# Dividing the attended rows instead of the probabilities, and copying the second tile's turned rows on VectorE

## The reference, cut to what matters

```python
m = jnp.max(s, -1, keepdims=True)
p = jnp.exp(s - m)
den = jnp.sum(p, -1, keepdims=True)
o = jnp.einsum('bdhnqk,bdhnkc->bdhnqc', (p / den).astype(v.dtype), vw)
```

## Time and profile before

| | us |
|---|---|
| median of 3 runs | 2731.94 |
| the three runs | 2727.18, 2731.94, 2734.06 |
| the profiled execution | 2726.64 |
| its span, first to last instruction | 2724.8 |

### The profile page before, as it was taken

How to read it: one execution, slowest core, us unless ns; L and a number is a source line. 1 busy time by engine, 2 the same in 40 slices (tenths; PEclk the granted TensorE clock), 3 DMA queues, 4 the chain that set the end, 5 groups by cost and what they waited for, 6 DMA issues and landing times.

```text
span 2724.8 us, 49556 instructions
## 1 busy us (share of the span) xinstructions
PE 2635.3 (97%) x20658; PEld 2060.4 (76%) x20658; DVE 1841.1 (68%) x2227; ACT 1556.5 (57%) x1989; POOL 228.5 (8%) x217
## 2 busy tenths in 40 slices
PE   8999999996799999999999999999999999999997
PEld 8898777774677777777777777777777777777765
DVE  4331388757777677767766776777677667767788
ACT  3102488621566666666666666666666666666663
POOL 0100132000000000000000000000001000000044
PEclk9999999998899999999999999999999999999998
DMA  5100233334679788878768797888787687878895
GB/s 187 32 32 25 72 86 110 102 117 154 227 278 314 272 285 298 307 269 321 273 258 300 284 315 267 285 294 304 273 321 280 257 296 282 310 272 285 299 338 210
DMA packets 299003, 646.50 MB, mean 237 GB/s; under 512 B 22899, under 2 KB 72499, under 8 KB 298739
## 3 DMA queue, kind: packets, MB, share of 16 engines
q1 hardware_dynamic: 288124, 610.95, 62.1%
q0 software_dynamic: 9024, 26.87, 3.6%
q10 hardware_dynamic: 1632, 5.51, 0.5%
HBM read 607.34 MB, written 26.28 MB: 233 GB/s over the span
## 4 chain that ended last, share of the span: by engine, by line
PE 90%; DVE 6%; issue 2%; ACT 1%; DMA 0%; POOL 0%; DVEq 0%; SPq 0%; ACTq 0%; POOLq 0%
PE banks L903 17%; PE banks L580 14%; PE banks L860 12%; PE banks L861 12%; PE banks L862 12%; PE banks L879 11%; PE banks L916 5%; DVE w_parts L1253 2%; PE banks L702 1%; PE banks L891 1%; PE banks L717 1%; DVE scored L1328 1%; ACT probs L1040 1%; PE banks L676 0%; PE banks L830 0%
## 5 line engine op out<-in xcount | busy, mean ns | idle before, releaser
L1253 DVE TENSOR_TENSOR w_parts<-raw_units,w_parts 128x1024 fp32r<-128x1024 f32 x1056 | 1273.0, 1226 | 445.4 <-ACT w_parts L1197 410.5
L1197 ACT CAST w_parts<-raw_units 128x1024 fp32r<-128x1024 f32 x1056 | 1101.9, 1052 | 543.7 <-PE banks L862 262.0
L860 PE MATMUL banks<-w_parts,xs_parts 128*128 128x512 f32 x1408 | 562.6, 400 | 4.7 <-DVE w_parts L1253 4.0
L861 PE MATMUL banks<-w_parts,xs_parts 128*128 128x512 f32 x1408 | 549.9, 391 | 0.0
L862 PE MATMUL banks<-w_parts,xs_parts 128*128 128x512 f32 x1408 | 549.6, 390 | 0.0
L903 PE MATMUL banks<-w_parts,h_parts 128*128 128x512 f32 x2112 | 498.3, 393 | 0.8 <-DVE w_parts L1253 0.8
L903 PEld LDWEIGHTS banks<-w_parts,h_parts 128*128 128x128 f32 x2112 | 391.4, 188 | 90.9 <-issue 10.0
L860 PEld LDWEIGHTS banks<-w_parts,xs_parts 128*128 128x128 f32 x1408 | 264.7, 188 | 82.9 <-issue 25.5
L879 PE MATMUL banks<-raw_units,xs_short 128*32 128x256 f32 (+1 forms) x6144 | 317.5, 362 | 0.0
L862 PEld LDWEIGHTS banks<-w_parts,xs_parts 128*128 128x128 f32 x1408 | 264.8, 188 | 56.9
L861 PEld LDWEIGHTS banks<-w_parts,xs_parts 128*128 128x128 f32 x1408 | 265.2, 188 | 51.2
(11 more groups left out here) (207 smaller groups left out, 2119.8 us busy)
## 6 DMA issues: line engine op xcount, KB each, us to landing
raw_units<-in_w_gate SPq DMA_DIRECT2D x352, 512.0 KB, 8.8
raw_units<-in_w_up SPq DMA_DIRECT2D x352, 512.0 KB, 9.7
raw_units<-in_w_down SPq DMA_DIRECT2D x352, 512.0 KB, 8.0
win_raw<-in_w_in SPq DMA_DIRECT2D x10, 1024.0 KB, 5.3
relT<-rel_bias SPq DMA_DIRECT2D x8, 960.0 KB, 4.5
x_rows<-x SPq DMA_DIRECT2D x10, 512.0 KB, 2.6
acc_rows<-ax SPq DMA_DIRECT2D x10, 512.0 KB, 2.8
fin<-acc_rows POOLq DMA_DIRECT2D x10, 512.0 KB, 8.0
```

Of the source, the lines that this page charges most:

```text
L860: nc.tensor.matmul(out, xs_parts[:, HI, k, :], w_hi, start=k == 0, stop=False)
L861: nc.tensor.matmul(out, xs_parts[:, LO, k, :], w_hi, start=False, stop=False)
L1197: nc.scalar.copy(w_parts[:, HI, n % SPLIT, :], raw[:, n % RING, :]).then_inc(s_hi, 1)
L1253: return nc.vector.tensor_tensor(out, whole, high.bitcast(F32), ALU.subtract)
```

## The change

The exponentials are turned as they are. For each round VectorE inverts the two columns of sums and writes each inverse 64 times beside itself (`invert`, 128x128), TensorE turns that tile in one transpose into bank 7 (`turn_inverse`), which puts the inverse of each query on the partitions of its tile, and ScalarE copies it to SBUF (`over_copy`). The copy of the attended rows becomes a multiplication by it. The short tile has the same three steps of its own. VectorE copies the turned second tile (`second_copy`); ScalarE keeps the first and the short one. The short scores share bank 7 with the turned inverses, so they move behind the low scores and wait for `over_copy` of round R-2.

```diff
-            def normalise_probs(n, parts):
-
-                width = (L_SAMPLE, L_PROMPT)[parts - 1]
-                dve.wait_ge(s_probs, n + 1)
-                if n >= 2:
-                    dve.wait_ge(s_soft, n - 1)
-                r = rden[:, n % 2 * 2:n % 2 * 2 + parts]
-                link(nc.vector.reciprocal(r, den[:, n % 4 * 2:n % 4 * 2 + parts]))
-                for j in range(parts):
-                    pr = probs[n % 4][:, j * width:(j + 1) * width]
-                    ins = nc.vector.tensor_scalar(pr, pr, r[:, j:j + 1], None, ALU.mult)
-                ins.then_inc(s_soft, 1)
+            def invert(R):
+
+                dve.wait_ge(s_probs, tile_no(R, 1) + 1)
+                nc.vector.reciprocal(inv_den.rearrange("p (i c) -> p i c", c=HD),
+                                     den[:, 2 * (R % 2):2 * (R % 2) + 2].unsqueeze(2).to_broadcast([P, 2, HD])).then_inc(s_inv, 1)
...
+            def second_copy(R):
+                n = tile_no(R, 1)
+                dve.wait_ge(s_pt, n + 1)
+                if n >= 4:
+                    dve.wait_ge(s_pv, group_of[n - 4] + 1)
+                b = bank_pair["turned", n]
+                nc.vector.tensor_copy(probsT[n % 4][:, :, :], psum[:, b:b + 2, :].rearrange("p b (k c) -> p (b k) c", c=P)).then_inc(s_ptd, 1)
...
-                    nc.vector.tensor_copy(attT[HD * (h % 2):HD * (h % 2) + HD, h // 2, t0:t0 + P],
-                                          psum[HD * i:HD * i + HD, bank, c0:c0 + P]).then_inc(s_att, 1)
+                    t0, rows = (first_tile + i) * P, slice(HD * i, HD * i + HD)
+                    nc.vector.tensor_tensor(attT[HD * (h % 2):HD * (h % 2) + HD, h // 2, t0:t0 + P], psum[rows, bank, c0:c0 + P],
+                                            scale[rows, :], ALU.mult).then_inc(s_att, 1)
...
             for R in range(ROUNDS):
                 add_bias(R, 0)
-                if R >= 1:
-                    normalise_probs(tile_no(R - 1, 1), 1)
                 add_bias(R, 1)
-                if short_scored_in(R - 1):
-                    normalise_probs(short_no((R - 1) // PAIRS), PT)
...
-                normalise_probs(tile_no(R, 0), 1)
+                if short_scored_in(R - 1):
+                    invert_short((R - 1) // PAIRS)
+                if R >= 1:
+                    invert(R - 1)
+                    second_copy(R - 1)
...
-            normalise_probs(tile_no(ROUNDS - 1, 1), 1)
+            dve.wait_ge(s_turned, ROUNDS - 1)
+            invert(ROUNDS - 1)
             short_attended(HEADS - 1)
             cat_low(0)
+            second_copy(ROUNDS - 1)
             wout_low(5)
```

On TensorE and ScalarE:

```diff
+                if r == SHORT_ROUND:
+                    parts_ready(h, 0)
...
+                    if R >= 2:
+                        pe.wait_ge(s_over, R - 1)
...
+            def turn_inverse(R):
+
+                pe.wait_ge(s_inv, R + 1)
...
+                nc.tensor.transpose(psum[:, inverse_bank(R), 0:P], inv_den, ident).then_inc(s_turned, 1)
...
             for R in range(ROUNDS):
+                if short_scored_in(R - 3):
+                    turn_short_inverse((R - 3) // PAIRS)
+                if R >= 2:
+                    turn_inverse(R - 2)
                 scores(R)
...
             values(ROUNDS - 2)
+            turn_inverse(ROUNDS - 1)
             values(ROUNDS - 1)
...
+            def over_copy(R):
+
+                act.wait_ge(s_turned, R + 1)
+                if R:
+                    act.wait_ge(s_att, taken_out[group_of[tile_no(R - 1, 0)]] + 2)
+                nc.scalar.copy(over_den, psum[:, inverse_bank(R), 0:P]).then_inc(s_over, 1)
...
+                if short_scored_in(R - 3):
+                    over_short_copy((R - 3) // PAIRS)
+                if R >= 2:
+                    over_copy(R - 2)
                 if R < ROUNDS:
                     exponent(tile_no(R, 0))
...
                     probs_copy(tile_no(R - 1, 0), KT)
-                    probs_copy(tile_no(R - 1, 1), KT)
                 if R < ROUNDS - 1:
                     exponent(tile_no(R, 1))
...
+            over_copy(ROUNDS - 1)
             act.wait_ge(s_wout, 32)
```

More of the change, by code:

```diff
@@ L322, in short_no, with copied, inverse_bank, round_of @@
             return PER_HEAD * h + 2 * SHORT_ROUND + 2
+        SECOND = {tile_no(R, 1): R for R in range(ROUNDS)}
+        def copied(eng, n):
+            if n in SECOND:
+                eng.wait_ge(s_ptd, SECOND[n] + 1)
+            else:
+                eng.wait_ge(s_ptc, 1 + sum(m not in SECOND for m in range(n)))
+        def inverse_bank(R):
+            return bank_pair["turned", tile_no(R, 0)] if R == ROUNDS - 1 else 7
+        def round_of(n):
+            return SECOND[n] if n in SECOND else SECOND[n + 1]
+        def den_cols(n):
+            if n in SECOND or n + 1 in SECOND:
+                return 2 * (SECOND.get(n, SECOND.get(n + 1)) % 2) + (n in SECOND)
+            return 4
         def short_scored_in(R):
@@ L655, in pair_free @@
                     what, n = used_before[use]
-                    pe.wait_ge(s_scored if what == "scores" else s_ptc, n + 1)
+                    if what == "scores":
+                        pe.wait_ge(s_scored, n + 1)
+                    else:
+                        copied(pe, n)
                 return bank_pair[use]
@@ L677, in scores @@
                                          k_high[h % 2][:, c * 512:c * 512 + 512], start=True, stop=False)
[L678 to L689, removed]
                 for c in range(2):
@@ L696, in scores @@
                 last.then_inc(s_qk, 1)
+                if r == SHORT_ROUND:
+                    parts_ready(h, 0)
+                    if h < 2:
+                        pe.wait_ge(s_zero, h + 1)
+                    if h:
+                        pe.wait_ge(s_scored, short_no(h - 1) + 1)
+                    if R >= 2:
+                        pe.wait_ge(s_over, R - 1)
+                    for j in range(PT):
+                        q0 = parts_col(j * P)
+                        out, q = psum[:, 7, j * L_PROMPT:(j + 1) * L_PROMPT], q_parts[h % 2][:, q0:q0 + P]
+                        nc.tensor.matmul(out, q, k_high[h % 2][:, OF_PIECE[0]], start=True, stop=False)
+                        last = nc.tensor.matmul(out, q, k_low[h % 2][:, OF_PIECE[0]], start=False, stop=True)
+                    last.then_inc(s_qk, 1)
             def turn_probs(n, blocks):
-                pe.wait_ge(s_soft, n + 1)
+                pe.wait_ge(s_probs, n + 1)
                 b = pair_free(("turned", n))
@@ L722, in short_values @@
                 n = short_no(h)
-                pe.wait_ge(s_ptc, n + 1)
+                copied(pe, n)
                 if h == HEADS - 1:
```

56 lines of the change are left out of this document (45 added, 11 removed).

## The result

The changed kernel took 2740.04 us (median of 6 runs, 2738.96 to 2742.36). The kernel before took 2728.28 us beside it (2726.64 to 2734.06). The ratio is 1.0042, 95% interval 1.0030 to 1.0054: slower by 0.4%, 11.8 us. The forecast was 2727, range 2719 to 2735, so the time lies above the range, at the place of the third rival (2741). The forecast's 2727 is 4.8 under the 2731.94 of the three earlier runs; from the 2728.28 of all six, 4.8 less is 2723.5, and the third rival's 8.8 more is 2737. The profiled execution has a span of 2737.2 us, 12.4 more than before.

What follows compares the result with a forecast made beforehand. TensorE was taken to bound the kernel, with 1.75 us per head of waits, VectorE being late. Attention body -5.0, start -0.6 and end +0.8 gave -4.8 us, from 2731.9 to 2727; range 2719 to 2735.

Steps and rivals of the forecast that it cites:

- the third rival: VectorE's reciprocal takes several cycles a column, 1.2 us for 128 columns; +8.8 us, 2741; chance 0.12.
- Five reciprocals of 128 columns instead of one or two: On VectorE per head, each reciprocal of 128 columns was priced at 0.29 us, from 1 ns per added column.
- Does VectorE keep up?: Timetable of a long round: inverse ready at 5.15 us, wanted by TensorE at 5.59, slack 0.4, so VectorE is off the path.
- The sum: TensorE's attention stage, first values to those of round 30: 189.8 us before, 184.8 after, a gain of 5.0.
- the 38 lone transposes: TensorE's added transposes of the inverses, at the pace of 0.12 us each, 4.6 us together.
- The tail: End of the attention stage: the low parts start 5.2 us after the last values instead of 4.4, 0.8 lost.
- The start: First values of the attention come 0.6 us earlier, as one scaling and reciprocal ahead of the first transposes goes.
- The short scores' wait: In r=1 TensorE's short scores wait 0.75 us for ScalarE's copy of the turned inverse, seven times, 5.3 us.
- The first rival: The wait of TensorE's short scores for ScalarE does not bite; -10.1 us, 2722; chance 0.22.
- The large copy: VectorE's four copies per head of the turned second tile out of PSUM, 1.15 us each, with nobody waiting for them.
- The second rival: TensorE's lone transposes cost their whole 0.3 us each, 6.8 us more; +2.0, 2734; chance 0.12.
- The fourth rival: TensorE still waits about as long per head, for ScalarE's first-tile copy or split parts; 0 to -2, 2731; chance 0.09.

Runs made afterwards that it cites:

- run 10: The same kernel as run 6, timed again on another chip; 2721.45 us, ratio 0.9974 to the kernel before.
- run 7: The kernel of run 2 with both turned tiles copied by ScalarE; 2745.58 us, ratio 1.0072 to the kernel before.
- run 2: The changed kernel with the sums inverted in two columns and then spread by a copy; 2730.83 us, ratio 1.0007 to the kernel before.
- run 3: The changed kernel with the long tiles' wide reciprocal placed ahead of the attended rows; 2732.30 us, ratio 1.0013 to the kernel before.
- run 6: The changed kernel with two-column reciprocals and spreading copy, lone transpose behind the scores except in r=1, small copy ahead of the split of k; 2725.12 us, ratio 0.9989.
- run 1: The kernel before with reciprocals of 1 to 128 columns and a spreading copy added ahead of its first work; 2738.58 us, run once.
- run 4: The kernel of run 2 with ScalarE's copy of the turned inverse ahead of its split of k; 2727.55 us, ratio 0.9992 to the kernel before.
- run 5: The changed kernel, reciprocals still wide, with the lone transpose behind its round's scores except in r=1; 2730.48 us, ratio 1.0010 to the kernel before.
- run 8: The kernel before, probabilities still scaled, with VectorE copying the turned second tile; 2743.98 us, ratio 1.0056.
- run 9: The kernel of run 6 with the inverse also taken ahead of the attended rows; 2722.09 us, ratio 0.9975 to the kernel before.

## Why the prediction was wrong

**What bounds the kernel** was read rightly: TensorE, with 1.75 us per head of waits for VectorE. The two waits that the change aimed at are gone from the heads in the profile after, and run 10 shows nearly no idle TensorE left in the stage.

**The step that failed** is "Five reciprocals of 128 columns instead of one or two ... 127 more columns at 1 ns give 0.29 us". It measured 0.95. The row behind it was read at one and two columns, from one instruction each, whose spread of 147 to 166 ns hides a step of 6. The prediction named that possibility, priced it as the third rival at 1.2 us, and gave it 0.12 because of that row. The row could not speak against it. The Trainium skill (VectorE: DVE Perf Modes, "First, the fixed hardware budget") calls the reciprocal an iterative divide with a repeat count of 8. Read as several steps for each column, as the rival read it, that pointed the right way; the measured slope is 6.25 ns a column where the rival took 8.3. A price bounded from both sides, 0.16 and 1.2 us with no row near 128 columns, should have carried the range up to 2741.

**Does VectorE keep up?** The timetable had the inverse ready at 5.15 us of a round against 5.59. With 0.95 for 0.3 that slack of 0.4 is a lack of 0.2, and behind the pair of 1.2 (4.85 + 1.9 - 5.59). Measured: 0.6, 0.5 and 1.3. The two small ones the third rival had put at "0.5 late or less" and left out of its price. Part of that was made up by its pair, 1.7 where 1.3 was measured. In all its +8.8 falls 3 us short of the measured +11.8; that its 2741 met the 2740 is luck, for it stood on 2731.94, 3.7 above the 2728.28 beside the result.

**The sum.** The body, first values to those of round 30, was forecast 5.0 shorter and came out 9.5 longer (526.55 - 327.26 = 199.3 against 189.8). Of the error of 14.5 the 22 waits ahead of lone transposes are 18.1 (from the sixteen transposes to the lone one 57.2 in all, less 22 x 1.78). Taken off are 1.8 for the short scores (3.5 above their pace in seven heads, where 5.3 stood), 1.2 for the 38 lone transposes (3.3 for 4.6), and 0.6 for small differences of pace. The tail, forecast +0.8, is +1.1 (532.09 - 526.55 = 5.54 against 4.4). Start and tail are in the profile after as:

```profile
324.42 0.95 DVE L1433 RECIPROCAL inv_den<-den 128x128 f32<-128x128 f32 x1
325.42 0.33 PE L747 MATMUL banks<-ident,inv_den 128*128 128x128 f32 x1 [1.12 <-DVE inv_den L1433]
...
526.55 1.97 PE L767 MATMUL banks<-probsT,v_rows 128*64 128x128 f32 x32
...
532.09 4.63 DVE L1332 TENSOR_TENSOR wout_parts_back<-wout_raw,wout_parts_front 128x1024 fp32r<-128x1024 f32 x4 [0.32 <-ACT wout_parts_front L1137]
```

The start had the wrong sign: first values forecast 0.6 earlier, 1.05 later (327.26 against 326.21). The first inverse stands on VectorE behind the biases of round 1 and the short ones, and the lone transpose stands in front of the scores of round 2, so the first values wait for a chain that before did not lie ahead of them. The prediction followed only the scaling that disappears. TensorE's clock was half for some us there (last section), but that is not the cause: in run 7 it stayed at full speed, with the same order of inverse and scores, and the first values came at 327.38. In all, +1.05 + 9.5 + 1.1 = 11.7 of the span's 12.4.

**The other terms held.** The short scores' wait of 0.75 is 0.95 where nothing else covers it (run 2); in the change itself the late inverse covers it, so the two did not add up. The first rival, that this wait does not bite, thus looks right in the change (0.2 us idle), but for another reason than its own, and it gave no gain. The large copy's record is 1.22 us, its spacing in run 3 1.14 (408.77 to 409.91) for 1.15, and no wait for it is listed in a period that long. The second rival, 0.3 us for each lone transpose, falls where the change puts it (0.06 to 0.18, pace taken 0.12), and is nearly right behind the scores (0.25 to 0.33). The fourth rival fell: the waits moved to another cause.

**The claim of the change** holds once its reciprocals are narrow, the lone transpose stands behind the scores and the small copy ahead of the split of k: 2.0 us faster in run 6 and 6.3 in run 10 by the medians, the same kernel, where 4.8 was forecast for the change. From the 2740.04 of the change, the narrow reciprocal is worth 9 us, the other two together another 6 (run 6) to 9 (run 10). Not tried were other orders for the first two rounds, where run 10 still has its first values 0.9 us later than before (327.13), 0.5 of it because its first scores begin later (314.98 for 314.50).

## What to carry to other kernels

An operation that a trace shows only at one or two columns gives no slope: measure it at the width that the change gives it, or carry the whole bound into the range. A broadcast source does not make a reciprocal cheap; invert the few values and spread them with a copy. And when work leaves a late engine, ask of each small result that stays on it (here the inverse) who stands directly behind it: the same wide reciprocals made this kernel 12 us slower than before in one order and some 3 us in two others.

## What the hardware did that was not expected

VectorE's reciprocal costs 6.25 ns a column from two columns on, spread source or not (run 1: 166 ns at 2, 953 at 128).

VectorE's 128-column copy from SBUF to SBUF takes longer beside GpSimd's subtractions. In runs 2, 4 and 10 the 78 spreading copies that began with no subtraction running took 0.226 to 0.231 us. The 42 that began during one took 0.23 to 0.73, and 39 of them ended 0.08 to 0.09 us after the end of that subtraction (in run 2 at 407.90 after 407.81). The copies out of PSUM beside subtractions stayed at 1.22, the wide reciprocals at 0.95. In the kernel before, the scaling of 1024 columns from SBUF to SBUF took 0.75 us alone and up to 1.29 beside them (325.17 us), so part of the load that the change removes was this. That is read from rows; no run took the subtractions away. The Trainium skill (SBUF — State Buffer, "Who interferes with whom") says that a VectorE copy in a mode that uses two ports shares a port pair with GpSimd, and that whichever instruction comes first holds the pair to its end while the other waits. This case's rows agree.

TensorE's granted clock fell to the lower level, 1.2 GHz, for some microseconds at the start of the attention in some profiles. The window table of the profile after, with the same columns:

```profile
316.00:320.00 4.00, 1.91 (x10) 0.89 (x8) 3.83 (x9) 2.64 (x4) 0.00 (x0) 1.00 0.95 316
320.00:324.00 4.00, 4.00 (x23) 3.80 (x20) 2.65 (x5) 3.95 (x8) 1.61 (x3) 0.57 0.76 211
```

TensorE had been idle for 2.09 us, waiting for the bias, and the sixteen transposes behind its next scores took 3.08 us instead of 1.98. In runs 2, 4, 5, 6, 8 and 9 the clock also fell after that pause, in run 4 only after a second one of 2.6 us. The kernel before and runs 3, 7 and 10 had the same pause of 2.09 us and stayed at 1.00 from 316 to 332 us. Runs 6 and 10 are the same kernel, one on each side, so it is a matter of the execution or the chip; which executions it takes is open. In runs 7 and 8 it fell again within the heads, behind waits of TensorE; before, in the change and in run 10 it stayed at 1.00 from 332 to 516 us.
